# Rows of x and memory loaded features first; value projections ahead of the norm factors; one queue for the first loads

## The reference, cut to what matters

```python
def rmsnorm(x, g):
    xf = x.astype(jnp.float32)
    r = lax.rsqrt(jnp.mean(xf * xf, axis=-1, keepdims=True) + EPS)
    return (xf * r * g.astype(jnp.float32)).astype(x.dtype)

def first_block(x, mix_pre_g, w_in, ...):
    h = rmsnorm(x, mix_pre_g[l])
    proj = h @ w_in[l]
    u, v_s, q, k, v_a, g_a, g_b, f_logit = jnp.split(proj, IN_SPLITS, axis=-1)
    y_a = spatial_gating(jax.nn.gelu(u), jax.nn.gelu(v_s), ...)
    y_b = forgetting_attention(q, k, v_a, f_logit, b_forget[l])
    merged = jax.nn.sigmoid(g_a) * y_a + jax.nn.sigmoid(g_b) * y_b
    x = x + rmsnorm(merged @ w_out[l], mix_post_g[l])
    h = rmsnorm(x, ffn_pre_g[l])
    x = x + rmsnorm(swiglu(h, w_gate[l], w_up[l], w_down[l]), ffn_post_g[l])
```

## Time and profile before

| | us |
|---|---|
| three runs | 1484.83, 1488.76, 1488.99; median 1488.76 |
| the profiled execution | 1486.36 |
| its span, first to last instruction | 1484.6 |
| TensorE busy (matmul) | 1147.1, 77% of the span |
| VectorE / ScalarE / GpSimd busy | 468.4 / 398.3 / 74.1 |
| moved by DMA | 503.33 MB |

### The profile page before, as it was taken

One profiled execution on the slowest core, in us unless ns is written; L12 is line 12 of the kernel. 1 busy time (PEld: TensorE's weight loads), 2 busy tenths in 40 slices (PEclk: granted clock), 3 DMA queues, 4 the chain that ended last, 5 costly groups with the idle time before them and its releaser, 6 DMA issues.

```text
span 1484.6 us, 19383 instructions
## 1 busy us (share of the span) xinstructions
PE 1147.1 (77%) x8336; PEld 754.3 (51%) x8336; DVE 468.4 (32%) x954; ACT 398.3 (27%) x890; POOL 74.1 (5%) x89
## 2 busy tenths in 40 slices
PE   9999999999999998995566466566665564565677
PEld 7888988888877875442322223223222232232234
DVE  6575777656788764110000000000000000000002
ACT  5665567555657642110000000000000000000002
POOL 0000020000035411000000000000000000000000
PEclk9999999999999998798778778787887787887789
DMA  8435546555553488999999999999999999999996
GB/s 313 171 138 203 198 172 223 208 207 199 199 187 114 149 347 343 397 436 434 433 437 426 433 433 435 424 442 430 430 437 426 438 430 433 433 426 440 423 424 288
DMA packets 29450, 503.33 MB, mean 339 GB/s; under 512 B 4275, under 2 KB 4915, under 8 KB 8245
## 3 DMA queue, kind: packets, MB, share of 16 engines
q1 hardware_dynamic: 25344, 493.43, 79.7%
q10 hardware_dynamic: 4020, 8.66, 1.6%
HBM read 501.03 MB, written 1.05 MB: 338 GB/s over the span
## 4 chain that ended last, share of the span: by engine, by line
issue 60%; PE 32%; DVE 5%; ACT 1%; POOL 1%; POOLq 0%; DVEq 0%; ACTq 0%
PE PB L378 9%; PE PB L358 5%; PE PB L359 5%; PE PB L360 5%; PE PB L379 4%; DVE SPL L1575 1%; DVE XN L1595 0%; PE PB L409 0%; POOL SP L2238 0%; PE PB L815 0%; PE PB L680 0%; PE PB L418 0%; PE PB L507 0%; PE PB L799 0%; PE PB L454 0%
## 5 line engine op out<-in xcount | busy, mean ns | idle before, releaser
L919 PE MATMUL PB<-RING,XS 128*32 128x512 f32 x2048 | 292.8, 720 | 177.0 <-DMA RING<-in_wgu_dram 176.7
L919 PEld LDWEIGHTS PB<-RING,XS 128*32 128x32 f32 x2048 | 68.4, 126 | 345.3 <-issue 249.8
L951 PE MATMUL PB<-RING,HHT 128*32 128x256 f32 x2048 | 150.9, 452 | 111.9 <-DMA RING<-in_wdn_dram 110.5
L1575 DVE TENSOR_TENSOR SPL<-RAW,SPH 128x512 fp32r<-128x512 f32 x318 | 207.0, 709 | 31.4 <-ACT SPH L1048 28.7
L378 PE MATMUL PB<-XT,SPH 128*128 128x512 f32 x544 | 194.1, 401 | 0.0
L1048 ACT ACTIVATE SPH<-RAW 128x512 fp32r<-128x512 f32 x340 | 186.8, 620 | 7.4 <-DMA RAW<-in_wst_dram 3.3
L951 PEld LDWEIGHTS PB<-RING,HHT 128*32 128x32 f32 x2048 | 75.3, 129 | 172.2 <-issue 141.7
L379 PE MATMUL PB<-XT,SPL 128*128 128x256 f32 x544 | 152.4, 280 | 0.0
L1506 ACT ACTIVATE SG<-PB 128x512 f32<-128x512 f32 x16 | 9.6, 597 | 506.1 <-PE PB L919 506.1
L2128 DVE SCALAR_TENSOR_TENSOR YL<-PB,COLS,YH 128x256 fp32r<-128x256 f32 x64 | 31.0, 484 | 279.0 <-ACT YH L1520 279.0
L378 PEld LDWEIGHTS PB<-XT,SPH 128*128 128x128 f32 x544 | 102.2, 188 | 24.6
(11 more groups left out here) (398 smaller groups left out, 1577.5 us busy)
## 6 DMA issues: line engine op xcount, KB each, us to landing
RAW<-in_wst_dram SPq DMA_DIRECT2D x84, 1024.0 KB, 4.9
RING<-in_wgu_dram SPq DMA_DIRECT2D x13, 2048.0 KB, 40.4
RING<-in_wgu_dram SPq DMA_DIRECT2D x4, 4096.0 KB, 22.3
RING<-in_wgu_dram SPq DMA_DIRECT2D x14, 1024.0 KB, 8.1
RING<-in_wdn_dram SPq DMA_DIRECT2D x6, 2048.0 KB, 13.4
RING<-in_wdn_dram SPq DMA_DIRECT2D x2, 4096.0 KB, 19.0
RING<-in_wdn_dram SPq DMA_DIRECT2D x3, 1024.0 KB, 41.0
RAW<-in_wst_dram SPq DMA_DIRECT2D x4, 256.0 KB, 5.6
```

Of the source, the lines that this page charges most:

```text
L919: i = e.matmul(PB[b][32 * c:32 * c + 32, :], XS[x % 2][:, k, :], chunk_at(n)[:, 512 * c:512 * c + 512], start=k == 0, stop=k == KD - 1)
L951: w = e.matmul(PB[b][32 * j:32 * j + 32, 0:T], HHT[:, j, 32 * c:32 * c + 32], chunk_at(n)[:, T * (4 * (c % 2) + j):T * (4 * (c % 2) + j + ...
L1575: e.tensor_tensor(l, src, h.bitcast(F32), ALU.subtract).then_inc(*lo.up())
```

## The change

x is also given features first: `xt` holds for each of 128 partitions the eight feature blocks of both row tiles, `XR` on chip; the memory rows come features first only, and the gain as a column, `GCOL`. The transposes of x at the start and of the memory rows are gone.

XR is multiplied by the gain in four quarters (one on VectorE, three on GpSimd) and split into XRH and XRL. The values of both halves are multiplied first, from these rows without the norm factor, and the factor is applied as the scale of their eviction (`values_out`). x in row-major form is loaded after that, only for the mean squares; TensorE spreads the two factors over the partitions (`norm_factors`, between row tiles of unit 1), VectorE scales XR by them, ScalarE and VectorE split it into XTH and XTL for all that follows. On ScalarE the eviction of the second half of the values now stands behind eight high parts, and the nine DMA issues (forget weights to PIOTA, unchanged) behind the split of the normed rows.

The first loads, but the gain and the identity, go through SyncE's queue in order of need; the units are reordered to match (values 0 to 3, queries 4 and 5, keys 6 and 7). Warm-up matmuls: 13 instead of 7 and 2. The order of the first output row tile becomes: blocks 0 to 4 of the first column half, 0 to 4 of the second, then 5 to 7 of each.

```diff
-U_VA, U_Q, U_K = (0, 6), (2, 8), (4, 10)
+U_VA, U_Q, U_K = (0, 2), (4, 8), (6, 10)
...
+    GCOL = place("GCOL", [P, KD], F32, SMALL + 144)
+    XR = place("XR", [P, 2, KD, P], F32, at(135))
+    XRL = place("XRL", [P, KD, T], F32R, at(159))
+    XRH = place("XRH", [P, KD, T], F32R, at(167))
...
-        for _ in range(7):
+        for _ in range(13):
             e.matmul(PB[4][:, 0:P], WARM[:, :], WARM[:, :], start=True, stop=True)
-        e.wait_ge(s_row, 16)
-        for i in range(2):
-            e.matmul(PB[6 + i][:, :], WARM[0:1, :], GROW[:, halves[i]], start=True, stop=True).then_inc(*mixd.up(("gain", i)))
-        for _ in range(2):
-            e.matmul(PB[4][:, 0:P], WARM[:, :], WARM[:, :], start=True, stop=True)
-        e.wait_ge(s_id, 16)
-        turn_tile(XN, 0, (0, 1), [vec.at(("n_in", 0, j)) for j in range(2)], None, "in")
-
-
-        def second_tile():
-            turn_tile(XN, 1, (0, 1), [vec.at(("n_in", 1, j)) for j in range(2)], [vec.at(("xt_in", 0, j)) for j in range(2)], "in")
-
-        rtile(U_VA[0], 2, 0, [("xt_in", 0, j) for j in range(2)], ("va", 0, 0), between=second_tile)
-        rtile(U_VA[0], 3, 1, [("xt_in", 1, j) for j in range(2)], ("va", 0, 1))
-        free = {0: vec.at(("xt_in", 1, 0)), 1: vec.at(("xt_in", 1, 1)), 2: act.at(("va", 0, 0)), 3: act.at(("va", 0, 1))}
+
+
+        def norm_factors():
+            e.wait_ge(s_id, 16)
+            for t in range(2):
+                e.wait_ge(*gps.at(("r", f"x{t}")))
+                r = e.matmul(PB[6][:, tiles[t]], rn[f"x{t}"].to_broadcast([P, P]), ident, start=True, stop=True)
+            r.then_inc(*mixd.up("r_in"))
+
+        for half_ in range(2):
+            for j in range(2):
+                for t in range(2):
+                    for k in range(4):
+                        if half_ == 0 and k == 0:
+                            e.wait_ge(*vec.at(("xr", t, j)))
+                        i = rk(U_VA[half_] + j, k, 4 * j + k, 2 - 2 * half_ + t, XRH, XRL, t, j + k == 0, j == 1 and k == 3)
+                    if j or t:
+                        i.then_inc(*prod.up(*([("va", half_, t)] if j else []), *([("unit", U_VA[half_] + j)] if t else [])))
+                    if (half_, j, t) == (0, 1, 0):
+                        norm_factors()
+        free = {b: act.at(("va", int(b < 2), b % 2)) for b in range(4)}
+        for j in range(2):
+            e.wait_ge(*vec.at(("xt_in", j)))
...
-            if half_:
-                for t in range(2):
-                    e.wait_ge(*free[t])
-                    rtile(U_VA[1], t, t, [("xt_in", t, j) for j in range(2)], ("va", 1, t))
-                    free[t] = act.at(("va", 1, t))
...
-        e.wait_ge(s_mem, 16)
-        for t in range(2):
-            for j in range(2):
-                b = 2 * t + j
-                e.wait_ge(*free[b])
-                for k in range(4 * j, 4 * j + 4):
-                    i = e.transpose(PB[b][:, (k % 4) * P:(k % 4 + 1) * P], MEM[:, t, k * P:(k + 1) * P], ident)
-                i.then_inc(*turn.up(("mem", t, j)))
-
         def out_tile(t):
-            for n in range(2):
-                for k in range(8):
+            order = [(n, k) for n in range(2) for k in range(8)] if t else [(n, k) for ks in (range(5), range(5, 8)) for n in range(2) for k in ks]
+            for n, k in order:
                     u = U_OUT + 2 * n + k // 4
                     if t == 0 and n == 0:
...
+        turn_tile(XN, 0, (0, 1), [vec.at(("n_ffn", 0, j)) for j in range(2)], [free[j] for j in range(2)], "ffn")
+        e.wait_ge(*vec.at(("memt", 3)))
...
-        e.dma_start(X[:, 0, 512:1024], io["x"][0:P, 512:1024]).then_inc(s_x[1], 16)
-        e.dma_start(GROW[:, :], io["mix_pre_g"].rearrange("(a n) -> a n", a=1)).then_inc(s_row, 16)
+        e.dma_start(GCOL[:, :], io["mix_pre_g"]).then_inc(s_gcol, 16)
+        e.wait_ge(*gps.at("mh"))
+        e.activation(first_act, MH[:, 0:1], ACT.Square).then_inc(*act.up())
...
+        def high_rows(t, j):
+            at_ = vec.at(("xg", 0, 0)) if t + j == 0 else gps.at(("xg", t, j))
+            e.wait_ge(*at_)
+            e.activation(XRH[:, 4 * j:4 * j + 4, tiles[t]], XR[:, t, 4 * j:4 * j + 4, :], ACT.Copy).then_inc(*act.up(("xr", t, j)))
+
+        high_rows(0, 0)
+        high(4)
+        high_rows(1, 0)
+        e.dma_start(CON[:, 0:128], io["con"][:, 0:128]).then_inc(s_id, 16)
+        high_rows(0, 1)
+        high(4)
+        high_rows(1, 1)
         squares_in(0, 0, "x0", (s_x[0], 16))
-        high(2)
-        for j in range(2):
-            high_turned(0, j, j, XTH, turn.at(("in", 0, j)), "xt_in")
-        high(2)
-        pre_squares(1, "x1", [(s_x[2], 16)] * 2)
+        squares_in(1, 0, "x1", (s_x[1], 16))
         high(4)
         for j in range(2):
-            high_turned(1, j, j, XTH, turn.at(("in", 1, j)), "xt_in")
-        high(8)
+            e.wait_ge(*vec.at(("n_in", j)))
+            e.activation(XTH[:, 4 * j:4 * j + 4, :].rearrange("p k (t c) -> p k t c", t=2),
+                         XR[:, :, 4 * j:4 * j + 4, :].rearrange("p t k c -> p k t c"), ACT.Copy).then_inc(*act.up(("xt_in", j)))
+        high(4)
...
-            e.activation(VA[:, t, halves[half_]], PB[bank][:, :], ACT.Copy).then_inc(*act.up(("va", half_, t)))
+            e.activation(VA[:, t, halves[half_]], PB[bank][:, :], ACT.Copy, scale=rn[f"x{t}"]).then_inc(*act.up(("va", half_, t)))
...
+        for t in range(2):
+            e.wait_ge(*gps.at(("r", f"x{t}")))
+        for t in range(2):
+            values_out(0, t)
+        high(8)
+        for t in range(2):
+            values_out(1, t)
         for half_ in range(2):
-            for t in range(2):
-                values_out(half_, t)
...
-            if half_ == 0:
-                high(8)
...
-        for t in range(2):
-            for j in range(2):
-                high_turned(t, j, 2 * t + j, MEMH, turn.at(("mem", t, j)), "memt")
+        e.wait_ge(s_mem, 16)
+        for q in range(4):
+            e.activation(MEMH[:, 2 * q:2 * q + 2, :], MEM[:, 2 * q:2 * q + 2, :], ACT.Copy).then_inc(*act.up(("memt", q)))
...
-        def first_norm(t, name):
-            e.wait_ge(*gps.at(("r", name)))
-            for h in range(2):
-                c = halves[h]
-                if t == 0:
-                    e.wait_ge(*mixd.at(("gain", h)))
-                e.scalar_tensor_tensor(out=XN[:, t, c], in0=X[:, t, c], scalar=rn[name], in1=PB[6 + h][:, :], op0=ALU.mult, op1=ALU.mult).then_inc(*vec.up(("n_in", t, h)))
-
-        e.wait_ge(s_x[1], 16)
-        e.tensor_tensor_reduce(XN[:, 0, halves[1]], X[:, 0, halves[1]], X[:, 0, halves[1]], 1.0 / D, 0.0, ALU.mult, ALU.add, ss["x0"][1]).then_inc(*vec.up())
-        mean_square("x0", act.at(("x0", 0)), vec.so_far())
-        first_norm(0, "x0")
-        low(2)
+        def low_rows(t, j):
+            e.wait_ge(*act.at(("xr", t, j)))
+            e.tensor_tensor(XRL[:, 4 * j:4 * j + 4, tiles[t]], XR[:, t, 4 * j:4 * j + 4, :], XRH[:, 4 * j:4 * j + 4, tiles[t]].bitcast(F32),
+                            ALU.subtract).then_inc(*vec.up(("xr", t, j)))
+
+        e.wait_ge(s_gcol, 16)
+        e.wait_ge(s_xt[0], 16)
+        e.tensor_tensor(XR[:, 0, 0:4, :], XR[:, 0, 0:4, :], GCOL[:, 0:4].unsqueeze(2).to_broadcast([P, 4, P]), ALU.mult).then_inc(*vec.up(("xg", 0, 0)))
+        low_rows(0, 0)
+        low(4)
+        low_rows(1, 0)
+        low_rows(0, 1)
+        low(4)
+        low_rows(1, 1)
+        for t in range(2):
+            e.wait_ge(s_x[t], 16)
+            e.tensor_tensor_reduce(XN[:, t, halves[1]], X[:, t, halves[1]], X[:, t, halves[1]], 1.0 / D, 0.0, ALU.mult, ALU.add, ss[f"x{t}"][1]).then_inc(*vec.up())
+        for t in range(2):
+            mean_square(f"x{t}", act.at((f"x{t}", 0)), vec.so_far())
+        low(4)
+        e.wait_ge(*mixd.at("r_in"))
         for j in range(2):
-            low_turned(0, j, j, XTH, XTL, "xt_in")
-        low(2)
-        mean_square("x1", act.at(("x1", 1)))
-        first_norm(1, "x1")
-        low(4)
+            scaled_rows = XR[:, :, 4 * j:4 * j + 4, :].rearrange("p t k c -> p k t c")
+            factors = PB[6][:, 0:T].rearrange("p (t c) -> p t c", t=2).unsqueeze(1).to_broadcast([P, 4, 2, P])
+            e.tensor_tensor(scaled_rows, scaled_rows, factors, ALU.mult).then_inc(*vec.up(("n_in", j)))
         for j in range(2):
-            low_turned(1, j, j, XTH, XTL, "xt_in")
-        low(8)
+            e.wait_ge(*act.at(("xt_in", j)))
+            e.tensor_tensor(XTL[:, 4 * j:4 * j + 4, :].rearrange("p k (t c) -> p k t c", t=2), XR[:, :, 4 * j:4 * j + 4, :].rearrange("p t k c -> p k t c"),
+                            XTH[:, 4 * j:4 * j + 4, :].rearrange("p k (t c) -> p k t c", t=2).bitcast(F32), ALU.subtract).then_inc(*vec.up(("xt_in", j)))
+        low(12)
...
-        for t in range(2):
-            for j in range(2):
-                low_turned(t, j, 2 * t + j, MEMH, MEML, "memt")
+        for q in range(4):
+            e.wait_ge(*act.at(("memt", q)))
```

(32 more changed lines are left out.)

21 lines of the change are left out of this document (8 added, 13 removed).

## The result

| | before | after |
|---|---|---|
| median of 20 runs each, us | 1486.89 (1484.69 to 1489.87) | 1489.05 (1487.13 to 1491.9) |
| mean | 1487.02 | 1489.01 |
| profiled execution, span | 1486.36, 1484.6 | 1489.42, 1487.6 |

The ratio is 1.0014, 95% interval 1.0008 to 1.0021: the changed kernel is slower by about 2.1 us (1.2 to 3.1). That is within 0.3%, but it is a difference that can be measured.

What follows compares the result with a forecast made beforehand. TensorE was taken to bound the first half (about 550 us), transfers at some 430 GB/s the rest. Start -1.1 and middle +1.8 gave +0.7 us, added to a mean of 1487.2: 1487.9 us, 80% range 1483.5 to 1491.5.

Steps and rivals of the forecast that it cites:

- The middle: First row tile of the output projection: late GpSimd pieces 120 to 123 cost 1.8 us instead of 1.9 gained.
- The bound of 205.2: First row tile: its end at 205.2 us in the old order without transposes, five steps behind piece 123.
- The start: Up to the first query block: ScalarE's queue decides, 1.1 us gained; ends 4.0 gained and 2.5 lost.
- the forecast 35.1: Start: ScalarE's eviction of bank 0 done at 35.1 us, for which the first query block waits.
- The price that I put on GpSimd beside VectorE: Start: 1.2 us added to VectorE's residues for GpSimd's three gain multiplies; ends 0 and 3.4.
- 36.2: Start: comparison mark in us, the old first query block at 25.30 plus 10.9 for the values' second half.
- The base: Whole kernel: mean of four shown executions, 1487.2 us, 1.5 below their median, to which the sum was added.
- (a) to (c): Rivals: both places gain, 1481.3, 0.12; early unit 2, middle lost, 1486.0, 0.20; start as forecast, pieces on time, 1484.2, 0.08.
- (d): Rival, start: one queue carries the whole head, unit 2 lands at 22, block at 38.7, total 1491.5; chance 0.14.
- The sum: Whole kernel: -1.1 at the start and +1.8 in the middle, +0.7 us in all.

Runs made afterwards that it cites:

- memory_alone: Kernel before with features-first memory rows, their transposes gone and the new order of the first row tile, old start kept; ratio to the kernel before 1.0009.
- plain_order: Changed kernel with the first output row tile in its old order, eight blocks of each column half in turn; ratio to the kernel before 1.0005.
- early_split: Changed kernel with ScalarE's high parts of pieces 120 to 123 made among the last four u blocks; ratio to the kernel before 1.0001.
- two_queues: Changed kernel with quarters two to four of the features-first rows issued by ScalarE behind GCOL; ratio to the kernel before 1.0029.
- start_alone: Changed kernel's start with the old memory rows, transposes and order; ratio to the kernel before 1.0011.
- the three edits: Changed kernel: DMA issues before the copies, factor matmuls 12 value matmuls later, second-half value evictions between two groups of four high parts; ratio to before 1.0007.
- before_again: The kernel before, unchanged, profiled once more for a second look at its start; time 1486.24 us.
- before_warm: Kernel before with 13 warm-up matmuls ahead of the gain row in place of 7; ratio to the kernel before 0.9996.
- before_look2: The kernel before, unchanged, profiled for a third look at its start; time 1488.73 us.
- before_look3: The kernel before, unchanged, profiled for a fourth look at its start; time 1486.88 us.

## Why the prediction was wrong

**The middle was right.** Forecast 1.8 us lost, four waits on GpSimd, 14.7 us from the last u block; measured 1.81, four, 14.72, and the same in memory_alone. The bound of 205.2 for the old order came out as 205.29. The edit that asks for the pieces later (plain_order) and the one that forms them earlier (early_split) each give the loss back.

**The start is the term that was mis-sized:** -1.1 worked out, -0.26 between the two profiled executions, about +0.4 against the mean of five old starts. Its steps held as mechanisms: first matmul 7.00 (6.9, where the terms as written add up to 6.75), a wait for the factors, then ScalarE's queue up to the eviction at 35.01 (34.5), for which the block waits. What failed is their time. The block came at 35.94, 0.84 behind the forecast 35.1, and most of that arose in ScalarE's queue: the nine issues took 4.93 us (24.63 to 29.56) in place of 4.5, and the block starts 0.93 behind the start of the eviction, where I counted 0.6. The loads cost little of it: unit 2 came at 19.16 (18.5), but VectorE's two scalings took 2.35 us (2.7), so they ended at 24.59 (24.4) and the issues began at 24.63 (24.5).

TensorE's own part was late by more: the factors were in PSUM at about 21.5 (19.7) and its values ended at about 34.9 (33.4). That goes back mostly to unit 1, at 13.28 (11.7), and here a row was misread. I put the longest RAW load of the earlier trace rows, 11.7 us, down to unit 2. It was issued behind 24 us; units 1 and 2 of before, issued at 4.08 and 4.88, landed 9.1 and 10.7 us later (first two lines), so at 13.2 and 15.6 and not at 12.2 and 16.1. Through these points unit 1 of the changed kernel comes at 12.4. The other 0.9 us goes with a lower rate, 264 GB/s from 2.5 to 7.5 us where before had 294 (last two lines, before first); no run isolates it.

```profile
RAW<-in_wst_dram SPq DMA_DIRECT2D x1, 1024.0 KB, 9.1
RAW<-in_wst_dram SPq DMA_DIRECT2D x1, 1024.0 KB, 10.7
```

```profile
2.50:7.50 5.00, 5.00 (x13) 2.79 (x12) 1.60 (x4) 2.17 (x5) 0.55 (x1) 1.00 0.93 294
2.50:7.50 5.00, 4.32 (x24) 4.11 (x23) 2.62 (x4) 2.44 (x6) 0.00 (x0) 1.00 0.87 264
```

The price that I put on GpSimd beside VectorE was 1.2 us; the rows give 3.34 against 2.50 for four residues alone, 0.84. The Trainium skill (SBUF — State Buffer, "SBUF: two separate sides") would have the residues lose the multiply's whole time, an estimate of 1.04 us by the first multiply, which ran with VectorE idle; 0.84 were lost, so the trace agrees in kind.

**The old start was one execution.** 36.2 was taken as a fixed number. It is one of 34.0 to 37.2, and what differs is the rate at which TensorE runs its gain row and first value matmuls: a slow clock, which I had weighed at the start of the changed kernel alone. The rows at 0.42 us were seen, but not asked whether they are the same each time.

**The base.** I added +0.7 to a mean of four executions, 1.5 below the shown median, and so wrote a number on the other side of that median than the sum. The mean was the better estimate of the kernel (20 runs: mean 1487.02, median 1486.89), but the forecast's direction was lost with it.

**The rivals.** (a) to (c) are out. (d), the one queue, has its beginning in the rows: units 1 and 2 came 1.6 and 0.7 us late. But unit 2 at 19.16 stays below the 19.6 at which the gain would be gone, and only about 0.1 of it reached ScalarE's issues. A second queue is no cure: two_queues has the ratio 1.0029 where the change has 1.0014.

**The sum, as it now stands:** +0.4 at the start and +1.8 in the tile are +2.2 beside +2.1 measured. The match is better than its parts: start_alone's timed ratio allows +0.3 to +3.0, and the marks' 0.4 lies near the low end of that. What it holds above stays open; the stretch from 470 to 592 us, in which the clock falls, differs by up to 3 us from one execution to the next, whatever the kernel.

## What to carry to other kernels

A transfer, copy or transpose that is taken away may have been the cover of a late piece: ask what the engines behind it were doing meanwhile, as GpSimd's four pieces show. Before a start is priced, read it in more than one execution, and give the forecast from the same base that the result is compared with. Where engines work in order, the edit of one late consumer may not show: the nine issues moved alone met a slow TensorE, and in their new place they held up the copy behind them; the factors moved alone gained nothing. Together the three edits brought the block 1.0 us forward, and only with the early pieces did the time fall below that of the kernel before.

## What the runs showed of the hardware

TensorE's clock at the start is not the same from one execution to the next: the same twelve matmuls of the kernel before stood 0.43 us apart for 8 to 11 of them, while memory_alone, with the same start, had 0.23 from the second on. The granted clock of the profile does not always show it: over such matmuls it reads 0.50 in before_again and before_warm, but 1.00 in before, before_look2 and before_look3, where only the distances tell. 13 warm-ups in place of 7 did not keep it at 2.4 GHz (before_warm). Moving three 256 KB loads to a second queue lowered the rate between 3 and 6 us from 220 to 302 down to 128 to 199 GB/s.
